# The second block's modulation product, moved into the first block's compression and retention stages and laid over four column groups of TensorE

## What is computed

```
s_lat = silu(c); s_ctx = silu(c_ctx)
for i in range(DEPTH):
    sh1, sc1, gt1, sh2, sc2, gt2 = split(s_lat @ ada_w[i] + ada_b[i], 6)
    sh1c, sc1c, gt1c, sh2c, sc2c, gt2c = split(s_ctx @ ada_w[i] + ada_b[i], 6)
    h = x * (1.0 + sc1) + sh1
    hc = ctx * (1.0 + sc1c) + sh1c
    ...
    x = layernorm(alpha * x + gt1 * y)
    x = layernorm(alpha * x + gt2 * swiglu(x * (1.0 + sc2) + sh2))
```

## Time and profile before

| | us |
|---|---|
| median of 3 runs | 5121.58 (5120.23 to 5123.51) |
| span of the profiled execution | 5116.2 |
| PE busy | 4404.1 (86%) |
| DVE busy | 2403.0 (47%) |
| ACT busy | 935.8 (18%) |
| POOL busy | 375.5 (7%) |

### The profile page before, as it was taken

One profiled execution on the slowest core, in us unless ns is written; L12 is line 12 of the kernel. 1 busy time (PEld: TensorE's weight loads), 2 busy tenths in 40 slices (PEclk: granted clock), 3 DMA queues, 4 the chain that ended last, 5 costly groups with the idle time before them and its releaser, 6 DMA issues.

```text
span 5116.2 us, 54474 instructions
## 1 busy us (share of the span) xinstructions
PE 4404.1 (86%) x21900; PEld 3539.9 (69%) x21900; DVE 2403.0 (47%) x3522; ACT 935.8 (18%) x1789; POOL 375.5 (7%) x302
## 2 busy tenths in 40 slices
PE   5989799889988999788879788869999689985997
PEld 4766588677666873578868788757879428654886
DVE  3423434534344352455546455564356624365346
ACT  1113100211221010232222222210020200240002
POOL 0000100000000000112210222010000010001000
PEclk8955799987559999899989888989999889997999
DMA  3200022211002226200001000212224351001222
GB/s 113 82 24 1 33 91 98 95 71 61 1 9 72 93 99 220 92 34 1 1 14 42 9 1 1 111 42 81 93 99 170 127 203 66 33 1 41 99 97 84
DMA packets 49774, 346.21 MB, mean 68 GB/s; under 512 B 5573, under 2 KB 6345, under 8 KB 10485
## 3 DMA queue, kind: packets, MB, share of 16 engines
q1 hardware_dynamic: 42336, 308.30, 17.0%
q10 hardware_dynamic: 7192, 34.42, 1.7%
HBM read 332.19 MB, written 10.51 MB: 67 GB/s over the span
## 4 chain that ended last, share of the span: by engine, by line
PE 73%; DVE 10%; DMA 7%; POOL 4%; issue 3%; ACT 2%; POOLq 1%; ACTq 0%; DVEq 0%; another core or an unknown queue 0%; SPq 0%
PE psum L468 16%; PE psum L469 15%; PE psum L470 15%; PE psum L1677 10%; DMA pieces_in<-pieces 6%; PE psum L1298 3%; PE psum L977 3%; PE psum L1001 2%; POOL xt_operands L618 2%; PE psum L987 2%; DVE pieces_lo L489 1%; POOL x_mem L1810 1%; PE psum L905 1%; PE psum L821 1%; PE psum L915 1%
## 5 line engine op out<-in xcount | busy, mean ns | idle before, releaser
L468 PE MATMUL psum<-xt_operands,pieces_hi 128*128 128x512 f32 (+1 forms) x2544 | 943.2, 371 | 109.8 <-DVE pieces_lo L489 107.8
L469 PE MATMUL psum<-xt_operands,pieces_hi 128*128 128x512 f32 (+1 forms) x2544 | 933.6, 367 | 0.0
L470 PE MATMUL psum<-xt_operands,pieces_lo 128*128 128x512 f32 (+1 forms) x2544 | 933.1, 367 | 0.0
L468 PEld LDWEIGHTS psum<-xt_operands,pieces_hi 128*128 128x128 f32 x2544 | 485.9, 191 | 194.7 <-DVE pieces_lo L489 112.3
L489 DVE TENSOR_TENSOR pieces_lo<-pieces_in,pieces_hi 128x2048 fp32r<-128x2048 f32 x240 | 549.8, 2291 | 6.5
L469 PEld LDWEIGHTS psum<-xt_operands,pieces_hi 128*128 128x128 f32 x2544 | 486.1, 191 | 79.3 <-issue 2.6
L470 PEld LDWEIGHTS psum<-xt_operands,pieces_lo 128*128 128x128 f32 x2544 | 485.4, 191 | 78.2
L482 DVE CAST pieces_hi<-pieces_in 128x2048 fp32r<-128x2048 f32 x240 | 292.8, 1220 | 269.7 <-PE psum L469 201.6
L618 POOL TENSOR_TENSOR xt_operands<-xt_values,xt_operands 128x512 fp32r<-128x512 f32 (+1 forms) x128 | 153.6, 1229 | 3408.4 <-DVE xt_operands L609 3408.4
L1183 DVE TENSOR_TENSOR arena<-psum,arena 128x512 f32<-128x512 f32 (+1 forms) x110 | 70.2, 638 | 652.0 <-ACT arena L1166 652.0
L468 PE MATMUL psum<-pieces_hi,xt_operands 128*128 128x512 f32 (+1 forms) x736 | 300.0, 408 | 73.6 <-DVE pieces_lo L489 73.6
(11 more groups left out here) (282 smaller groups left out, 5621.4 us busy)
## 6 DMA issues: line engine op xcount, KB each, us to landing
pieces_in<-pieces SPq DMA_DIRECT2D x294, 1024.0 KB, 4.8
arena<-ln ACTq DMA_DIRECT2D x4, 1024.0 KB
x_park<-x_mem ACTq DMA_DIRECT2D x1, 3072.0 KB, 11.9
o_park<-arena ACTq DMA_DIRECT2D x2, 1536.0 KB
arena<-o_park ACTq DMA_DIRECT2D x1, 3072.0 KB
x_mem<-x_park ACTq DMA_DIRECT2D x1, 3072.0 KB, 18.1
arena<-line ACTq DMA_DIRECT2D x6, 448.0 KB, 5.7
arena<-c ACTq DMA_DIRECT2D x1, 2304.5 KB, 14.7
```

The source lines that it names most:

```text
L468: signal_later(k, pe.matmul(out, sh, mh, start=start, stop=False))
L469: signal_later(k, pe.matmul(out, sh, ml, start=False, stop=False))
L470: return pe.matmul(out, sl, mh, start=False, stop=stop)
```

## The change

The weight pieces of `ada_w[l]` are put into layer l of the first block, behind the two pieces of compress (`layer_slabs`), in another layout: a piece now holds one 128-row tile and 2048 output columns. The new `ada_pe` multiplies a piece with four matmuls. Each has 32 stationary columns (the two conditions and 30 of zeros, `k.cond32`) and its own 512 moving columns, and writes its own 32 partitions of one PSUM bank. Six pieces are used in compress (two at each of three places) and three in each head of retention. DVE adds the bias for three groups of 2048 columns, ACT stores the sums to DRAM (`mods`). In the second block the two ada stages become `mods`: ACT loads the shifts and scales (two partitions) and the gate rows (four transfers that repeat a row for 128 partitions), PE does the 32 transposes, DVE the four additions. The number of pieces stays the same. ACT also loads the conditions and applies Silu in compress, and POOL zeroes `cond32` there.

```diff
+def compress_pool(k, e, _=None):
+    e.eng.memset(k.cond32, 0.0).then_inc(k.S.cond_padded, 1)
...
+def ada_pe(k, pe, slot, pieces):
+
+    S = k.S
+    for n in pieces:
+        group, kt = divmod(n, KT)
+        w = take_raw(k, pe, slot)
+        if kt == 0 and group == 2:
+            pe.wait_ge(S.ada_taken, 1)
+        for j in range(4):
+            last = pe.matmul(k.ps[32 * j:32 * j + 32, ADA_BANK[group], :], k.cond32[:, kt, :],
+                             w[:, 512 * j:512 * j + 512], start=kt == 0, stop=kt == KT - 1)
+            if j == 0:
+                signal_later(k, last)
+        piece_used(k, slot, split=False)
+        if kt == KT - 1:
+            last.then_inc(S.ada_ps, 1)
+
+
+def ada_take_dve(k, e, group):
+    dve, S = e.eng, k.S
+    dve.wait_ge(S.ada_ps, group + 1)
+    dve.wait_ge(S.ada_b_loaded, 16 * (group + 1))
+    dve.tensor_tensor(k.ada_out[group % 2], k.ps[:, ADA_BANK[group], :], k.ada_bias, ALU.add).then_inc(S.ada_taken, 1)
+
+
+def ada_store_act(k, e, group):
+    act, S, T = e.eng, k.S, k.T
+    act.wait_ge(S.ada_taken, group + 1)
+    act.dma_start(T["mods"][bass.ds(k.layer, 1), group].rearrange("a p n -> (a p) n"),
+                  k.ada_out[group % 2]).then_inc(S.spilled, 16)
+    if group < 2:
+        act.wait_ge(S.spilled, 16 * (group + 1))
+        ada_bias_act(k, e, group + 1)
...
@@ retention_pe, for each head
+        ada_pe(k, pe, slot, range(6 + 3 * h, 9 + 3 * h))
         if h:
             values(h - 1)
...
@@ retention_act
+    ada_bias_act(k, e, 0)
     for h in range(N_RET):
+        if h in (2, 5):
+            ada_store_act(k, e, h // 3)
         act.wait_ge(S.o_ps, h + 1)
...
@@ retention_dve
+        if h in (1, 4):
+            ada_take_dve(k, e, h // 3)
+    k.dve_piece += ADA_PIECES
+    ada_take_dve(k, e, 2)
...
+def mods_act(k, e, layer):
+    act, S, T = e.eng, k.S, k.T
+    mods = T["mods"]
+    at = layer * 3 * P * 512
+    act.dma_start(k.mods[0:2, :].rearrange("p (a b n) -> p a b n", b=4, n=512),
+                  bass.AP(mods.tensor, at, [[512, 2], [P * 512, 3], [32 * 512, 4], [1, 512]])).then_inc(S.mods_loaded, 16)
+    for n in range(4):
+        c = (2, 5)[n // 2] * 2
+        row = (c // 4) * P + 32 * (c % 4) + n % 2
+        act.dma_start(k.gt[:, n, :].rearrange("p (b n) -> p b n", n=512),
+                      bass.AP(mods.tensor, at + row * 512, [[0, P], [32 * 512, 2], [1, 512]])).then_inc(S.gate_rows_loaded, 16)
     if layer == 0:
...
+        act.wait_ge(S.loaded, 32)
+    act.wait_ge(S.gate_rows_loaded, 64)
```

More of the change, by code:

```diff
@@ L380, in _ @@
             with act.Fori(0, DEPTH) as layer:
+                k.layer = layer
                 act.dma_start(k.sm, T["small1"][bass.ds(layer, 1)].rearrange("a p n -> (a p) n")).then_inc(S.loaded, 16)
@@ L409, in _ @@
             with pool.Fori(0, DEPTH):
-                for stage_pool in (xt_pool, no_pool, no_pool, no_pool, no_pool, no_pool,
+                for stage_pool in (xt_pool, no_pool, no_pool, compress_pool, no_pool, no_pool,
                                    xt_pool, no_pool, xt_pool, no_pool):
@@ L826, in compress_pe @@
     last.then_inc(S.hid_ps, 1)
+    pe.wait_ge(S.cond_ready, 1)
+    ada_pe(k, pe, slot, range(0, 2))
     ws = cols(SM, k.sm, "ws", 4, P)
@@ L832, in compress_pe @@
                   k.tok[:, :, 2, 256 + 64 * g:320 + 64 * g], start=True, stop=True).then_inc(S.sv_ps, 1)
+    ada_pe(k, pe, slot, range(2, 4))
     pe.wait_ge(S.hid_ready, 2)
@@ L841, in compress_pe @@
     last.then_inc(S.kcv_ps, 1)
+    ada_pe(k, pe, slot, range(4, 6))
     pe.wait_ge(S.kc_sq, 1)
@@ L847, in compress_act @@
     act, S = e.eng, k.S
+    act.dma_start(k.cond, k.T["cond"]).then_inc(S.cond_loaded, 16)
+    act.wait_ge(S.cond_loaded, 16)
+    act.wait_ge(S.cond_padded, 1)
+    act.activation(k.cond32[:, :, 0:2], k.cond, ACT.Silu).then_inc(S.cond_ready, 1)
     v = k.tok[:, :, 2, 256:512]
@@ L892, in compress_dve, with ada_bias_act @@
                                     ALU.mult, ALU.mult))
+ADA_PIECES = 3 * KT
+ADA_BANK = (7, 6, 7)
+def ada_pe(k, pe, slot, pieces):
[26 more added lines that the diff above has]
+        ada_bias_act(k, e, group + 1)
+def ada_bias_act(k, e, group):
+    e.eng.dma_start(k.ada_bias, k.T["ada_b"][bass.ds(k.layer, 1), group].rearrange("a p n -> (a p) n")).then_inc(k.S.ada_b_loaded, 16)
 def retention_pe(k, e, slot):
@@ L1284, with mods_pe @@
 LAMBDA_INIT = 0.8 - 0.6 * math.exp(-0.3 * 1)
-def ada_pe(k, e, slot, _):
+def mods_pe(k, e, slot, _):
     pe, S = e.eng, k.S
[L1290 to L1303, removed]
+    pe.wait_ge(S.mods_loaded, 16)
     for i, w in enumerate((0, 1, 3, 4)):
@@ L1326, in ada_act, with mods_dve @@
         act.dma_start(k.c2, T["c2"]).then_inc(S.loaded, 16)
[L1327 to L1335, removed]
-    dve, S = e.eng, k.S
[L1337 to L1342, removed]
+        act.wait_ge(S.loaded, 32)
+    act.wait_ge(S.gate_rows_loaded, 64)
+def mods_dve(k, e, _):
+    dve, S = e.eng, k.S
     dve.wait_ge(S.tr_done, 1)
@@ L2293, in head_slabs, with ada_slabs, layer_slabs @@
             for c in range(0, w.shape[1], 512)]
-def layer_slabs(w_in, w_out, gate_up, w_down, w1):
+def ada_slabs(w):
+    wide = w.reshape(KT, P, 3, PIECE).transpose(2, 0, 1, 3).reshape(3 * KT // 2, 2, P, PIECE)
+    return [np.concatenate([s[0], s[1]], axis=1) for s in wide]
+def layer_slabs(w_in, w_out, gate_up, w_down, w1, ada):
     nq = [w_in[:, 1536 + 64 * h:1600 + 64 * h] for h in range(N_NSA)]
@@ L2308, in layer_slabs @@
     out.append(np.concatenate([one, one], axis=0))
+    out += ada_slabs(ada)
     out += chunk_slabs(w_out)
@@ L2426, in second_slabs @@
     w = v["dn_w_in_2"][0]
-    out = chunk_slabs(v["ada_w_2"][0])
+    out = []
     for half in range(2):
@@ L2439, in second_slabs, with ada_bias @@
     return out
+def ada_bias(b):
+    out = np.zeros((DEPTH, 3, 4, 32, 512), np.float32)
+    out[:, :, :, 0:2] = b.reshape(DEPTH, 3, 4, 1, 512)
+    return out.reshape(DEPTH, 3, P, 512)
 def kernel(**inputs):
@@ L2453 @@
     ln = np.stack([np.stack([v[f"ln{n}_g_2"][l], v[f"ln{n}_b_2"][l]]) for l in range(DEPTH) for n in (1, 2)])
-    sel = np.zeros((2, 2, P), np.float32)
-    sel[0, 0], sel[1, 1] = 1.0, 1.0
     lam = v["da_lambda_2"][0]
@@ L2472 @@
     T["line"] = nc.dram_tensor("line", (N_NSA, 1024), F32).ap()
+    T["mods"] = nc.dram_tensor("mods", (DEPTH, 3, P, 512), F32).ap()
     T["x_park"] = nc.dram_tensor("x_park", (P, NT2, D), F32).ap()
```

40 lines of the change are left out of this document (18 added, 22 removed).

## The result

| | before | after |
|---|---|---|
| median of the runs, us | 5120.9 (5116.84 to 5123.51, 4 runs) | 5054.35 (5052.82 to 5058.71, 4 runs) |
| ratio, 95% interval | | 0.9874 (0.986 to 0.9888) |
| span of the profiled execution, us | 5116.2 | 5056.8 |
| compress, layers 1 and 2, us | 37.68, 37.80 | 50.06, 49.09 |
| retention, us | 62.25, 62.26 | 111.72, 112.32 |

The kernel is 1.3% faster. The forecast was 5050 us. The page of the changed kernel has the same shape as the earlier trace rows: PE's share of the chain is two points lower, the DMA's one point higher.

What follows compares the result with a forecast made beforehand. PE was taken to bound the kernel, with no idle PE to fill in retention. Two layers at 60 us each less 191.8 us from the ada stages gave -71.8, so 5121.6 became 5050 us; range 5000 to 5078 (8 in 10).

Steps and rivals of the forecast that it cites:

- The price of a piece: Pieces in compression and retention: four column groups run at once, so a piece costs 1.9 us at half clock.
- Rival (a): In the pieces, records go in order, only two groups at a time: 3.6 us at half clock, 5006 us; chance 0.17.
- The ring: In each retention head, the third piece's slot is released late, so PE waits 3.1 us; three pieces take 8.8 us.
- Compression: Six pieces cost 11.4 us, some 1.5 more for landing, 0.8 less for a covered table load: 12.1 us added.
- The clock in retention: In retention heads the clock may rise and fall again, mostly staying at half: 3 us taken off a layer.
- The end of retention: At retention's end the last bias's load and addition make DVE's reduce start later: 1.3 us added.
- A layer: Time added to compression and retention together in each layer of the first block: 60 us.
- The mods stages: In the second block they replace the ada stages, ending with transfers at 333 GB/s: 15.0 and 9.6 us.
- The total: Whole kernel: two layers' additions less the ada stages' saving, -71.8 us on the span, giving 5050 us.
- rival (b): In the pieces, column groups run one behind the other at full clock: 57 us a layer, 5044 us; chance 0.05.

Runs made afterwards that it cites:

- e3: Changed kernel with only column groups 0 and 1 multiplied in 18 of 24 pieces a layer, half the matmuls left out there: 5058.42 us.
- e1: Changed kernel with a piece's slot released by its own last matmul (except three of 24 pieces), not by the next piece's first: 4987.5 us.
- e4: Changed kernel with the gate rows' transfers reading 128 different rows instead of one row 128 times (wrong gates): 5043.21 us, one run.
- e2: Changed kernel with all four matmuls on column group 0 in 21 of 24 pieces a layer (wrong modulation): 5048.63 us.
- e8: Kernel of e6 with the three pieces of a head spread: behind the second product, the fourth, and the values: 5014.57 us.
- e6: Changed kernel with the early slot release of e1, and mods stages that no longer wait for the gate rows: 4987.6 us.
- e9: The same kernel as e6, run again in five rounds: 4985.99 us.

## Why the prediction was right, and where its steps were off

- **The price of a piece** (1.9 us at half clock, four groups at once): 1.87 from start to start, 343.80 to 345.67. Right. Two groups take as long as four (e3). Rival (a) rested on an order by records, in which a group's second record holds up the next group's first; it falls, because four first records are running 0.05 us after the first began, and the second ones start 0.84 us later. The Trainium skill, TensorE: Matmul & The Clock Gate, in "Part 3: Packing small matmuls", says that matmuls start and end strictly in program order. Read for records, as the prediction read it, the trace doesn't agree, by the same 0.05 and 0.84 us; read for whole matmuls, each of two records, the windows here don't contradict it. The Trainium skill, TensorEngine Tiling (Array Packing), in "Theoretical Speedup", allows up to four times for 32 stationary columns. The trace agrees: by the earlier trace rows four matmuls one behind the other are 6.9 us at half clock, here they are 1.87, 3.7 times.
- **The ring** (3.1 us a head): heads 2 to 5 have one wait ahead of the third piece, 3.28 to 3.88 us. The third piece of the head shown starts 6.91 us after the first (336.89 to 343.80), 6.9 forecast, and the three take 8.8 us, 8.8 forecast. Head 1 has three waits, 5.07 us together (1.77, 1.42, 1.88), so a layer waits 19.2 us where 15.5 were forecast. e1 shows that the late release was the cause of most of it.
- **Compression** (+12.1): +12.4 and +11.3. The number is right, its terms are not, and that is luck. The sum had 1.5 us of waiting ahead of the last two pieces; layer 1 waits 5.9 us in three places, two of them here and 1.64 us ahead of the last piece:

```profile
291.62 1.07 PE L932 MATMUL psum<-pieces_in,xt_values 128*32 128x512 f32 x8 [1.83 <-DMA pieces_in<-pieces]
295.07 1.94 PE L932 MATMUL psum<-pieces_in,xt_values 128*32 128x512 f32 x8 [2.39 <-DMA pieces_in<-pieces]
```

What pays for it is the full clock behind the first pieces, which the sum had at half clock throughout: L844 is 1.8 us shorter than L831, the pieces are 1.4 us shorter than 11.4, and the products ahead of them end 0.7 us earlier than before.
- **The clock in retention** (-3): it gave some 3 us, as taken. It was at full from 314.7 to 321.6 us, behind head 0's three pieces, which come without a wait, and there L981 takes 2.42 us and a piece 1.06. In the later heads the three pieces lift it too late: it was at full twice more for 3.4 us, and these fell mostly on the wait itself:

```profile
314.70:321.60 6.90, 4.29 (x24) 1.58 (x16) 2.33 (x5) 0.00 (x0) 0.00 (x0) 0.99 0.78 304
376.20:379.60 3.40, 0.05 (x4) 0.00 (x0) 0.00 (x0) 0.00 (x0) 0.00 (x0) 1.00 0.92 376
393.20:396.60 3.40, 0.66 (x8) 0.00 (x0) 0.00 (x0) 0.00 (x0) 0.00 (x0) 0.99 0.78 275
```

- **The end of retention** (+1.3): nothing. I had DVE start its reduce late because of the last bias; but ACT issued that bias's load at 406.45, the bias was there at 409.05, and ACT's own squares on the way to the reduce ended after the addition. The mechanism was right and shows in e1, where the heads are short: the reduce comes 4.5 us later there. Rows of ACT and DVE at that place, against the earlier trace rows:

```profile
406.45 0.34 ACTq L959 DMA_DIRECT2D xt_values<-ada_b  x1
408.43 0.39 ACT L996 ACTIVATE xt_values<-psum 128x256 f32<-128x256 f32 x1 [3.88 <-PE psum L971]
408.85 1.49 ACT L999 ACTIVATE arena<-xt_values 128x1536 f32<-128x1536 f32 x1
...
409.05 0.69 DVE L945 TENSOR_TENSOR xt_values<-psum,xt_values 128x512 f32<-128x512 f32 x1 [17.95 <-DMA xt_values<-ada_b]
410.36 1.75 DVE L1022 TENSOR_REDUCE arena<-arena 128x24 f32<-128x1536 f32 x1 [0.62 <-ACT arena L999]
```

- **A layer** (60 us): 61.9 and 61.4. Waits 8 us longer than forecast (3.7 in retention, 4.4 in compression) are mostly made up by full clock in compression, which the sum didn't have, and by the +1.3 that didn't come. So here too luck has a part.
- **The mods stages** (15.0 and 9.6): 20.00 and 12.32. This is the term that was mis-sized, by 7.7 us. The step was to take 333 GB/s from the earlier trace rows, where the rows overlap but no row is read 128 times over. The price of repeated rows stood in the text only as a bound of 17 us. With distinct rows (e4) the stages are 15.82 and 9.76, within 0.8 and 0.2 us of the forecast.
- **The total.** In the spans, -59.4 us against -71.8 forecast: 7.7 from the mods stages, 3.2 from the two layers, 1.5 from stages not touched. In the medians only 4.4 are missing (5054.35 against 5050), since before's profiled execution lay 5.4 us under its median and after's lay 2.4 over it. So part of the closeness of 5050 is luck, on top of that within a layer.
- **What the forecast drew no conclusion from** is that the packing, at the release that the change has, buys nothing over one group (e2). Its own numbers said so, 5044 for rival (b) against 5050. I had written the full clock of rival (b) and the waits of the forecast side by side, found "by time it can't be told", and stopped there. It was the sign that the release was the thing to change.

## What to carry to other kernels

Look for the instruction that frees a ring's slot. Where it belongs to a later user of the ring, as here, a consumer that gets faster meets the transfer's whole latency (4.8 us, once in nearly every head); free the slot from the last instruction that reads it. The packing was worth its price here only together with what feeds it: -6 us before the release was moved, 46.5 after. And price a stage by clock and work together: a shorter product that leaves the engine at half clock gives up what its neighbours could have saved (products and values 4.6 and 4.5 us a head, against 2.4 each). Last, check each term of a sum, also where the total comes out: in compression two wrong terms cancelled.

## What the runs showed of the hardware that I had not expected

- Four column groups of float32 products with 32 stationary and 512 moving columns take the time of two (1.94 against 1.92 us at half clock).
- The same instructions of one loop ran one turn at a clock of 0.54 nearly without waits (95.13 us) and the other at 0.85 with waits (72.73 us), in one execution (e8). A stretch with PE busy for 30.00 of 30.00 us stayed at 0.50.
- One 2 KB row of DRAM read for 128 partitions was slower than 128 rows (changed kernel against e4, one execution each): the landing time of the slowest of eight such transfers is 13.0 us against 8.9, with nearly as many packets and bytes in the window (1668 and 1666, 4.93 and 4.90 MB).
- Untouched stages differ by up to 7 us from one execution to the next, with the granted clock (0.92 in the scan stage of 390.08 us, 0.91 in that of 397.35). A gain of 12.7 us in the stages where it was made (e6 and e9 against e1) could not be found in the medians.
